# Convolution layer's input projection as seven half-size products in twelve of sixteen blocks

## The chip, the cores and the metric

The kernel runs on one core of one Trainium2 chip. The metric is the device time of one execution in microseconds (us). TensorE (PE in the profile) multiplies, VectorE (DVE), ScalarE (ACT) and GpSimd (POOL) work element by element, and SyncE (SP) issues the transfers from HBM.

## The reference, cut to what matters

A model with d = 1024, an inner width of 2048 and 512 tokens runs through four mixers (pool, convolution, latent attention, pool) and then two attention and feed-forward layers. All is float32. The changed part is the input projection of the convolution mixer:

```python
def conv_mixer(xn, w_in, conv_w, w_out):
    b, c, h, z = jnp.split(xn @ w_in, 4, axis=-1)
    y = b * causal_depthwise_conv(c * h, conv_w)
    return (y * jax.nn.silu(z)) @ w_out
```

`xn` is the normed input (512 x 1024), `w_in` is 1024 x 8192, and b, c, h, z are 512 x 2048 each.

## The kernel before, in words

Activations are held feature-major: a tile is 128 features (partitions) by 512 tokens. A matrix product keeps float32 accuracy with three matmuls: each operand is split into a rounded high part (type fp32r) and a remainder, and `mm3` issues high x high, high x low and low x high into one PSUM bank.

The work is cut into **units**. A unit is one weight tile of 128 x 1024 float32 (512 KB): eight k-blocks of 128 x 128, for 128 output features. In the convolution layer, block i (of 16) makes 128 features of each of c, h, b and z with four units, `("cc", i)`, `("ch", i)`, `("cb", i)`, `("cz", i)`; each is eight k-steps of three matmuls 512 columns wide. Eight units of `out_proj("co", 0)` follow block 7, and eight of `out_proj("co", 1)` follow block 15.

Each engine runs its own program in a fixed order, and counting semaphores join them (`at(...)` names the result that is awaited, `mark(...)` the one that is announced). Four programs carry a unit's weights, each by a function `weights(n)` that makes every unit up to n in order:

- SP loads unit n into one of four `raw` tiles; it waits until the remainder of the unit that held the tile is made (`wlo`). SP's queue is in order.
- ACT copies `raw` to the high part `WH[n % 3]` (line 1133); it waits for the transfer and until PE has finished unit n - 3 (`wfree`), because there are three weight buffers.
- DVE subtracts, raw - WH, into `WL[n % 3]` (line 1837).
- PE waits for that before the unit's first matmul.

`taking(key)` calls `weights(unit[key] + 2)`: while PE works on unit n, ACT and DVE make unit n + 2. So the high part of unit n + 2 can begin when PE begins unit n, and whatever stands ahead of the call in the program of ACT or DVE comes first.

The element work of a convolution block: DVE makes CD = c x r^2 (r is the norm's factor per token), then `("ch", i)` = h x CD; ACT scales it by the third tap into CV; DVE adds the two shifted taps (`cv0`); POOL multiplies CV by r (`cv`, line 2759); DVE multiplies b in (`cb`), makes z x r (`czr`); ACT applies Silu; POOL multiplies the two (`czy`, line 2764); ACT and DVE split the result into `YH` and `YL` for the output projection. In block 1 to 3 DVE also makes the rotary angles (`positions`, `angle`), and ACT their sines in block 5.

A layer that comes later, the second feed-forward product (`quarter`), already uses seven products in place of eight, with `PRODUCTS`, `CHAIN_OF` and `ROWS_T`.

Of the kernel before, what the change touches and what calls it, by code (L numbers as in the profile page):

```python
# [9 lines left out]
F32R = mybir.dt.float32r  # L10
I32 = mybir.dt.int32
ALU = mybir.AluOpType
# [3 lines left out]
S = 512  # L16
# [55 lines left out]

FF_ORDER = (0, 4, 1, 5, 2, 6, 3, 7)
# [12 lines left out]
SEMS = ("xin0", "xin1", "xin2", "xin3", "xin4", "xin5", "xin6", "xin7", "consts", "vec", "raw0", "raw1", "raw2", "raw3", "pos", "lam", "cos", "sin", "fn", "out",  # L86
# [48 lines left out]
def unit_table(D):  # L135

    units, index, lows = [], {}, False

    def add(key, src, ncol, dup=False):
        index[key] = len(units)  # L140
        units.append([src, ncol, dup])
# [22 lines left out]
    for i2 in range(8):  # L164
        for i in (2 * i2, 2 * i2 + 1):
            for off, nm in ((16, "cc"), (32, "ch"), (0, "cb"), (48, "cz")):
                add((nm, i), D["conv_in"][0, off + i], 1024)
        if i2 % 4 == 3:
            out_units("co", D["conv_out"], i2 // 4)
# [53 lines left out]
    loaded = [n for n, u in enumerate(units) if not isinstance(u[0], tuple)]  # L223
    slots = {n: (i % NRAW, loaded[i - NRAW] if i >= NRAW else None) for i, n in enumerate(loaded)}
    return units, index, slots
# [75 lines left out]
def program(nc, D, out):  # L301
    ctx = ExitStack()
    with ctx:
        def sb(name, cols, dt=F32, parts=128):
            return ctx.enter_context(nc.sbuf_tensor(name, [parts, cols], dt))
# [24 lines left out]
        raw = [sb(f"raw{i}", WN) for i in range(NRAW)]  # L330
# [18 lines left out]
        units, unit, slots = unit_table(D)  # L349
# [63 lines left out]
        def weight_source(n):  # L413
            src, ncol = units[n][0:2]
            if isinstance(src, tuple):
# [15 lines left out]
        def pe_program(handle, c):  # L431
# [44 lines left out]
            def xgemm(st, *key, first=False, norm=None):  # L476
                gemm8(key, XH, XL, (lambda k: ("xl", st, k)) if first else None, norm)
# [100 lines left out]

            def conv_layer():
                for i2 in range(8):  # L580
                    for i in (2 * i2, 2 * i2 + 1):
                        xgemm(1, "cc", i, first=i == 0)
# [530 lines left out]
        def act_program(handle, c):  # L1113
# [127 lines left out]
            def conv_layer(done):  # L1241
                for i2 in range(8):
                    for i in (2 * i2, 2 * i2 + 1):
                        taking("cc", i)
                        if i == 0:
                            root(1, 1024)
                        taking("ch", i)
                        act.wait_ge(*at("ch", i))
                        if i > 1:
                            act.wait_ge(*at("cb", i - 2))  # L1250
                        act.do.activation(CV[i % 2], temp("ch", i), ACT.Copy, scale=vcol("conv_w2", i)).then_inc(
                            *mark("act", ("cv2", i)))
                        taking("cb", i)
                        taking("cz", i)
                        t = temp("cz", i)
                        act.wait_ge(*at("czr", i))
                        act.do.activation(t, t, ACT.Silu).then_inc(*mark("act", ("czs", i)))
                        y_high("co", i // 8, i % 8, t, ("czy", i))
                        if i == 5:
                            sines()  # L1260
                    if i2 % 4 == 3:
                        out_proj("co", i2 // 4, done if i2 == 7 else None)

# [548 lines left out]
        def dve_program(handle, c):  # L1812
# [64 lines left out]
            def out_proj(name, rb, st=None, first=0):  # L1877
                for m in range(first, 8):
                    taking(name, rb, m)
                    add_out(m, (name, rb, m), ("x", name, rb, m) if st is None else ("x", st, m))  # L1880
                    if st is not None and st != "mid" and st < 8:
# [76 lines left out]
            def conv_layer():  # L1958
                for i2 in range(8):
                    for i in (2 * i2, 2 * i2 + 1):  # L1960
                        taking("cc", i)
                        if i == 0:
                            recip_root(1, R[:, :])
                            dve.wait_ge(*mine())
                            dve.do.tensor_tensor(CR2, R[:, :], R[:, :], ALU.mult).then_inc(*mark("dve", ("r2",)))
                        dve.wait_ge(*at("mm", "cc", i))
# [9 lines left out]
                        a = CV[i % 2]  # L1976
                        dve.wait_ge(*at("cv2", i))
                        dve.do.scalar_tensor_tensor(a, shifted(("ch", i), 1), vcol("conv_w1", i), a, ALU.mult,
                                                    ALU.add).then_inc(*mark("dve"))
                        dve.wait_ge(*mine())  # L1980
                        dve.do.scalar_tensor_tensor(a, shifted(("ch", i), 2), vcol("conv_w0", i), a, ALU.mult,
                                                    ALU.add).then_inc(*mark("dve", ("cv0", i), ("tfree", "ch", i)))
                        taking("cb", i)
                        dve.wait_ge(*at("mm", "cb", i))
                        dve.wait_ge(*at("cv", i))
                        if i > 1:
# [6 lines left out]
                        low(YL[i % 8][:, :], t, YH[i % 8][:, :], ("yh", "co", i // 8, i % 8),  # L1993
                            ("yl", "co", i // 8, i % 8), ("tfree", "cz", i))
                        if i == 1:
                            positions()
                        if i == 2:
                            angle("sin", SIN[:, :], 0.0, 0.0)
                        if i == 3:
                            angle("cos", COS[:, :], 0.25, math.pi / 2)  # L2000
                    if i2 % 4 == 3:
                        out_proj("co", i2 // 4, 2 if i2 == 7 else None)
# [677 lines left out]
        def pool_program(handle, c):  # L2680
# [72 lines left out]
            def conv_layer():  # L2753
                for i2 in range(8):
                    for i in (2 * i2, 2 * i2 + 1):
                        taking("ch", i)
                        pool.wait_ge(*at("cv0", i))
                        pool.wait_ge(*at("rstd", 1))
                        pool.do.tensor_tensor(CV[i % 2], CV[i % 2], R[:, :], ALU.mult).then_inc(*mark("pool", ("cv", i)))
                        taking("cz", i)  # L2760
                        t = temp("cz", i)
                        pool.wait_ge(*at("czs", i))
                        pool.wait_ge(*at("cb", i))
                        pool.do.tensor_tensor(t, t, CB[i % 2], ALU.mult).then_inc(*mark("pool", ("czy", i)))
                        if i == 6:
                            pool.wait_ge(*at("sin"))
                            pool.do.tensor_scalar(SIN[:, :], SIN[:, :], const[:, C_SGN:C_SGN + 1], None,
                                                  ALU.mult).then_inc(*mark("pool", ("sinr",)))
                    if i2 % 4 == 3:
                        out_proj("co", i2 // 4, 2 if i2 == 7 else None)  # L2770
# [149 lines left out]
        def sp_program(handle, c):  # L2920
# [4 lines left out]
            def weights(n):  # L2925
                while made[0] <= min(n, len(units) - 1):
                    k = made[0]
                    made[0] += 1
                    src, ncol, _, _ = units[k]
                    if isinstance(src, tuple):  # L2930
                        continue
                    slot, before = slots[k]
                    if before is not None:
                        sp.wait_ge(*at("wlo", before))
                    sp.do.dma_start(raw[slot][:, 0:ncol], src).then_inc(*mark(f"raw{slot}", ("raw", k), by=16))
# [208 lines left out]
```

## Time and profile before

| | before |
|---|---|
| median of three runs | 2676.91 us (2676.52 to 2676.93) |
| profiled execution, its own time | 2678.12 us |
| span of its profile | 2676.3 us |
| mean granted TensorE clock | 0.998 |
| convolution layer's projection, one block | 21.76 us, 16 blocks |

The span goes from the first to the last instruction. Busy times of matmuls overlap, since matmuls are pipelined: the record of a 512-column matmul is 0.39 us long, but the next one starts 0.23 us after it. So the distance from start to start is what a matmul costs.

### The profile page before, as it was taken

The numbers are of one execution on the slowest core, as the hardware profiler recorded it, in microseconds if no ns is written. First come the engines' busy times: TensorE is split into PE (matmuls) and PEld (weight loads), VectorE is DVE, ScalarE is ACT, GpSimd is POOL, SyncE is SP. The second block draws the span as 40 slices with busy tenths as digits, with TensorE's granted clock in tenths as the row PEclk, the third lists the DMA queues.
The fourth block names the chain that finished last, engine by engine and source line by source line (L and its number), as shares of the span: only waits on it lengthen the run. The fifth ranks groups of instructions, "written<-read, shape, count | busy, mean of one in ns | idle before, by whom it ended". The sixth has DMA issues, their size and how long they took to land.

```text
span 2676.3 us, 32512 instructions
## 1 busy us (share of the span) xinstructions
PE 2652.0 (99%) x12772; PEld 2222.6 (83%) x12772; DVE 1703.9 (64%) x2604; ACT 1272.0 (48%) x2002; POOL 651.6 (24%) x688
## 2 busy tenths in 40 slices
PE   8999999999999999999999999999999999999998
PEld 7888888888888888888888888788888888788887
DVE  7656554344466646666574768776677468776677
ACT  4323332222346636533235677654445677654445
POOL 1000111011126626500003744420000554420000
PEclk9999999999999999999999999999999999999999
DMA  4222222222221222222222221354551221255540
GB/s 161 98 99 98 90 103 102 95 95 95 96 68 63 68 88 66 79 87 105 95 100 97 79 72 40 105 141 148 173 158 42 80 64 48 97 152 153 173 142 32
DMA packets 76841, 263.98 MB, mean 99 GB/s; under 512 B 8976, under 2 KB 11536, under 8 KB 76688
## 3 DMA queue, kind: packets, MB, share of 16 engines
q1 hardware_dynamic: 71568, 245.12, 26.7%
q0 software_dynamic: 5120, 16.78, 3.7%
q8 instruction: 101, 1.65, 0.2%
q14 instruction: 52, 0.43, 0.0%
HBM read 259.77 MB, written 2.10 MB: 98 GB/s over the span
## 4 chain that ended last, share of the span: by engine, by line
PE 91%; DVE 4%; ACT 2%; POOL 2%; issue 0%; DMA 0%; SPq 0%; ACTq 0%; DVEq 0%
PE ps L454 27%; PE ps L455 26%; PE ps L456 26%; PE ps L460 2%; PE ps L459 2%; PE ps L461 2%; POOL wl L2707 2%; PE ps L595 1%; PE ps L857 1%; PE ps L856 1%; DVE wl L1837 1%; ACT wh L1133 0%; DVE xl L1849 0%; PE ps L528 0%; ACT xh L1144 0%
## 5 line engine op out<-in xcount | busy, mean ns | idle before, releaser
L454 PE MATMUL ps<-xh,wh 128*128 128x512 f32 x1920 | 752.2, 392 | 0.1
L455 PE MATMUL ps<-xl,wh 128*128 128x512 f32 x1920 | 748.1, 390 | 0.0
L456 PE MATMUL ps<-xh,wl 128*128 128x512 f32 x1920 | 748.0, 390 | 0.0
L1133 ACT ACTIVATE wh<-raw 128x1024 fp32r<-128x1024 f32 (+3 forms) x389 | 397.6, 1023 | 474.4 <-PE ps L456 434.9
L454 PEld LDWEIGHTS ps<-xh,wh 128*128 128x128 f32 x1920 | 361.0, 188 | 77.0 <-issue 1.2
L456 PEld LDWEIGHTS ps<-xh,wl 128*128 128x128 f32 x1920 | 360.9, 188 | 75.3
L455 PEld LDWEIGHTS ps<-xl,wh 128*128 128x128 f32 x1920 | 361.0, 188 | 74.7 <-issue 1.0
L1837 DVE TENSOR_TENSOR wl<-raw,wh 128x1024 fp32r<-128x1024 f32 (+1 forms) x275 | 339.6, 1235 | 119.9 <-ACT wh L1133 119.9
L2707 POOL TENSOR_TENSOR wl<-raw,wh 128x256 fp32r<-128x256 f32 x408 | 315.3, 806 | 405.5 <-ACT wh L1133 405.5
L454 PE MATMUL ps<-yh,wh 128*128 128x512 f32 x640 | 251.1, 392 | 1.5 <-POOL wl L2707 1.5
L456 PE MATMUL ps<-yh,wl 128*128 128x512 f32 x640 | 249.2, 389 | 0.0
L455 PE MATMUL ps<-yl,wh 128*128 128x512 f32 x640 | 249.1, 389 | 0.0
L2716 POOL TENSOR_TENSOR acc<-acc,t 128x512 f32<-128x512 f32 x52 | 72.9, 1403 | 679.7 <-ACT t L1154 677.4
L1133 ACT ACTIVATE wh<-a 128x1024 fp32r<-128x1024 f32 x96 | 101.9, 1062 | 126.8 <-PE ps L456 64.4
L1845 DVE TENSOR_TENSOR yl<-t,yh 128x512 fp32r<-128x512 f32 (+1 forms) x148 | 101.5, 687 | 78.2 <-ACT yh L1142 78.2
L454 PEld LDWEIGHTS ps<-yh,wh 128*128 128x128 f32 x640 | 120.2, 188 | 28.6 <-POOL wl L2707 3.2
L456 PEld LDWEIGHTS ps<-yh,wl 128*128 128x128 f32 x640 | 120.1, 188 | 25.2
L1142 ACT ACTIVATE yh<-t 128x512 fp32r<-128x512 f32 (+1 forms) x148 | 86.4, 585 | 114.3 <-DVE t L1949 56.3
L455 PEld LDWEIGHTS ps<-yl,wh 128*128 128x128 f32 x640 | 120.2, 188 | 23.9
L1874 DVE TENSOR_TENSOR x<-ps,x 128x512 f32<-128x512 f32 x96 | 65.6, 688 | 116.9 <-PE ps L456 116.9
L1837 DVE TENSOR_TENSOR wl<-a,wh 128x1024 fp32r<-128x1024 f32 x96 | 117.3, 1221 | 32.1 <-ACT wh L1133 32.1
L2827 POOL DMA_DIRECT2D wsum<-in_ff2t x32 | 27.2, 976 | 328.7 <-DMA wsum<-in_ff2t 322.8
(307 smaller groups left out, 4755.3 us busy)
## 6 DMA issues: line engine op xcount, KB each, us to landing
raw<-in_pool_in SPq DMA_DIRECT2D x64, 512.0 KB, 3.2
raw<-in_conv_in SPq DMA_DIRECT2D x64, 512.0 KB, 3.2
raw<-in_ff SPq DMA_DIRECT2D x64, 512.0 KB, 6.2
a<-in_ff2t SPq DMA_DIRECT2D x64, 512.0 KB, 6.9
raw<-in_pool_out SPq DMA_DIRECT2D x32, 512.0 KB, 3.2
raw<-in_qk SPq DMA_DIRECT2D x32, 512.0 KB, 3.5
raw<-in_pool_grp SPq DMA_DIRECT2D x16, 512.0 KB, 3.2
raw<-in_conv_out SPq DMA_DIRECT2D x16, 512.0 KB, 3.2
```

Of the source, the lines that this page charges most:

```text
L454: pe.do.matmul(o, lh, rh_, start=start, stop=False)
L455: pe.do.matmul(o, lh, rl_, start=False, stop=False)
L456: return pe.do.matmul(o, ll, rh_, start=False, stop=stop)
L459: pe.do.matmul(o, lh, rh_, start=False, stop=False, skip_group_check=True)
L460: pe.do.matmul(o, lh, rl_, start=False, stop=False, skip_group_check=True)
L1133: act.do.activation(h[:, 0:ncol], r[:, 0:ncol], ACT.Copy).then_inc(*mark("whi", ("whi", k)))
L1142: act.do.activation(dst, src, ACT.Copy).then_inc(*mark("act", done))
L1837: dve.do.tensor_tensor(lo[:, 0:ncol], r[:, 0:ncol], f(h[:, 0:ncol]), ALU.subtract).then_inc(*mark("wlo", ("wlo", k)))
L1845: dve.do.tensor_tensor(dst, src, f(h), ALU.subtract).then_inc(*mark("dve", *done))
L1874: dve.do.tensor_tensor(x[m][:, :], ps(*key)[:, :], x[m][:, :], ALU.add).then_inc(*mark("dve", ("psfree",) + key, *done))
L2707: p = pool.do.tensor_tensor(lo[:, cc], r[:, cc], f(h[:, cc]), ALU.subtract)
L2716: pool.do.tensor_tensor(ACC[:, :], ACC[:, :], temp("sq", use, k), ALU.add).then_inc(*mark("pool", ("acc", use, k), ("tfree", "sq", use, k)))
```

## The change

In the blocks of `CONV_BLOCKS` (2 to 6, 8 to 14) the four units become two **pairs**, (c, h) and (b, z). A pair is a product with a 2 x 2 block structure: the weights are four pieces of 512 rows x 128 features, the activations four pieces of 512 features x 256 tokens. Seven products of half size replace eight. They use sums of weight pieces and sums of activation pieces:

- The activation sums are the same for all blocks. They are made once, in blocks 0 and 1, in four steps k: ACT scales two x tiles into `COS` and `SIN` (`x_scaled`), POOL makes four sums of 256 columns and a negation (`t_sums`), ACT and DVE split the 1024 columns (`t_high`, `t_low`) into `TC[k]`.
- The weight sums are made by POOL for each block and pair: four additions 512 columns wide (`w_sums`), one block ahead, into `SW[p]`.
- A pair's products come in four weight units: (Q1, Q2) from a raw tile, (Q6, W5) and (Q7, Q3) from the two halves of `SW[p]`, and Q4 from half a raw tile. Each product is four k-steps of three matmuls of 256 columns. The units of the two pairs alternate: eight weight units a block, called s0 to s7 below.
- Products accumulate in chains in PSUM (Q1, Q6, Q7, Q4 in one bank; W5, Q3 beside Q2 in another). Between them ACT copies out partial sums (`ca1`, `ca2`, `cc1`) and DVE adds (`third_sum`, `upper`), which gives c, h, b and z scaled (`lower`).
- Per block SP still loads four tiles of 512 KB. Two more raw tiles, `RX`, serve from block 3 to block 15.
- The tap, Silu and y work of such a block moves into the next block's steps. `positions` and `angle` move into `out_proj("co", 0)`, and the sines behind it.

```diff
+CONV_BLOCKS = (2, 3, 4, 5, 6, 8, 9, 10, 11, 12, 13, 14)
+CONV_PAIRS = ((16, 32), (0, 48))
+CONV_PARTS = (("Q1", "Q2"), ("Q6", "W5"), ("Q7", "Q3"), ("Q4",))
```

ACT's program for a block of seven products, and for blocks 0, 1, 7 and 15:

```diff
+            def seven(i):
+                late = i - 1 in CONV_BLOCKS
+                for s in range(8):
+                    if s == 1:
+                        first_sum(i, 0)
+                    if s == 2:
+                        first_sum(i, 1)
+                    if s in (3, 4):
+                        second_sums(i, s - 3)
+                    if late and s == 0:
+                        tap(i - 1)
+                    if late and s == 1:
+                        gate(i - 1)
+                    weights(unit["cp", i, s % 2, s // 2] + LOOK)
+                    if late and s == 4:
+                        y_out(i - 1)
...
+            def eight(i):
+                late = i - 1 in CONV_BLOCKS
+                taking("cc", i)
+                if i == 0:
+                    root(1, 1024)
+                if late:
+                    tap(i - 1)
+                    gate(i - 1)
+                if i == 1:
+                    t_high(1)
+                    x_scaled(2)
+                taking("ch", i)
+                if late:
+                    y_out(i - 1)
+                tap(i)
+                if i == 1:
+                    t_high(2)
+                    x_scaled(3)
+                taking("cb", i)
+                if i == 0:
+                    x_scaled(0)
+                taking("cz", i)
+                if i == 0:
+                    t_high(0)
+                    x_scaled(1)
+                if i == 1:
+                    t_high(3)
+                gate(i)
+                y_out(i)
```

DVE's program for a block of seven products:

```diff
+                def seven(i):
+                    late = i - 1 in CONV_BLOCKS
+                    for s in range(8):
+                        if late and s == 0:
+                            lower(i - 1, 1, 1)
+                            lower(i - 1, 1, 0)
+                        if late and s == 1:
+                            taps(i - 1)
+                        if late and s == 2:
+                            gated(i - 1)
+                        if s == 5:
+                            third_sum(i, 0)
+                            upper(i, 0)
+                            both_scaled(i)
+                        if s == 6:
+                            third_sum(i, 1)
+                            lower(i, 0, 1)
+                        if s == 7:
+                            lower(i, 0, 0)
+                            upper(i, 1)
+                        weights(unit["cp", i, s % 2, s // 2] + LOOK)
+                        if late and s == 4:
+                            y_out(i - 1)
```

POOL's weight sums, and its order:

```diff
+                def w_sums(i, p):
+                    s2, s1, s3, s4 = [SW[p][:, 512 * n:512 * n + 512] for n in range(4)]
...
+                    pool.do.tensor_tensor(s1, b[:, 0:512], b[:, 512:1024], ALU.add).then_inc(
+                        *mark("pool", ("ws1", i, p)))
...
+                    pool.do.tensor_tensor(s3, a[:, 0:512], b[:, 0:512], ALU.add)
+                    pool.wait_ge(*at("ws1", i, p))
+                    pool.do.tensor_tensor(s2, s1, a[:, 0:512], ALU.add).then_inc(*mark("pool", ("ws", i, p, 0)))
+                    pool.wait_ge(*at("ws", i, p, 0))
+                    pool.do.tensor_tensor(s4, s2, a[:, 512:1024], ALU.add).then_inc(*mark("pool", ("ws", i, p, 1)))
+
+                for i in range(16):
+                    if i - 1 in CONV_BLOCKS:
+                        taps(i - 1)
+                        gated(i - 1)
+                    if i not in CONV_BLOCKS:
+                        taps(i)
+                    if i < 2:
+                        t_sums(2 * i)
+                    if i == 1:
+                        t_sums(3)
+                    if i not in CONV_BLOCKS:
+                        gated(i)
+                    if i == 0:
+                        t_sums(1)
+                    if i + 1 in CONV_BLOCKS:
+                        for p in range(2):
+                            w_sums(i + 1, p)
```

## Rows read from the trace of the kernel before

**Rows 1.** The page, busy time of each engine over the span.
```profile
PE 2652.0 (99%) x12772; PEld 2222.6 (83%) x12772; DVE 1703.9 (64%) x2604; ACT 1272.0 (48%) x2002; POOL 651.6 (24%) x688
```

**Rows 2.** Windows: one convolution block; columns PE, PEld, DVE, ACT, POOL busy, clock, DMA.
```profile
599.36:621.12 21.76, 21.76 (x98) 18.02 (x97) 9.69 (x11) 6.01 (x7) 3.50 (x2) 1.00 0.28 97
```

**Rows 3.** Timeline, PE, matmuls of 512 columns: start, length, engine, line.
```profile
359.96 0.39 PE L454 MATMUL ps<-xh,wh 128*128 128x512 f32 x1
...
360.64 0.39 PE L454 MATMUL ps<-xh,wh 128*128 128x512 f32 x1
```

**Rows 4.** Timeline, PE, first and last of 36 matmuls of 256 columns.
```profile
1461.73 0.28 PE L454 MATMUL ps<-wh,xh 128*128 128x256 f32 x1
...
1465.93 0.28 PE L456 MATMUL ps<-wh,xl 128*128 128x256 f32 x1
```

**Rows 5.** Timeline at the start of a unit: PE's first matmul, then ACT, DVE.
```profile
207.13 0.39 PE L454 MATMUL ps<-g,wh 128*128 128x512 f32 x1
...
207.39 1.06 ACT L1133 ACTIVATE wh<-raw 128x1024 fp32r<-128x1024 f32 x1 [3.86 <-PE ps L456]
...
208.48 1.23 DVE L1837 TENSOR_TENSOR wl<-raw,wh 128x1024 fp32r<-128x1024 f32 x1 [0.46 <-ACT wh L1133]
```

**Rows 6.** Timeline, convolution block 1, from the end of ("ch", 1).
```profile
349.28 0.69 DVE L1974 TENSOR_TENSOR t<-ps,s 128x512 f32<-128x512 f32 x1 [2.71 <-PE ps L456]
350.00 0.72 ACT L1251 ACTIVATE s<-t,vec 128x512 f32<-128x512 f32 x1 [5.04 <-DVE t L1974]
...
351.55 0.75 DVE L1981 SCALAR_TENSOR_TENSOR s<-t,vec,s 128x512 f32<-128x512 f32 x1
352.21 1.22 DVE L1837 TENSOR_TENSOR wl<-raw,wh 128x1024 fp32r<-128x1024 f32 x1
352.38 2.21 POOL L2759 TENSOR_TENSOR s<-s,r 128x512 f32<-128x512 f32 x1 [10.43 <-DVE s L1981]
...
361.59 1.29 POOL L2764 TENSOR_TENSOR t<-t,s 128x512 f32<-128x512 f32 x1 [7.00 <-ACT t L1257]
```

**Rows 7.** Timeline, end of the first pool layer: GpSimd and VectorE together.
```profile
301.25 1.30 POOL L2716 TENSOR_TENSOR acc<-acc,t 128x512 f32<-128x512 f32 x1 [4.15 <-ACT t L1154]
...
301.82 1.28 DVE L1849 SCALAR_TENSOR_TENSOR xl<-x,vec,xh 128x512 fp32r<-128x512 f32 x1 [1.31 <-ACT xh L1144]
```

**Rows 8.** Timeline, first attention layer: GpSimd without a gap, VectorE behind it.
```profile
1501.64 2.83 POOL L2707 TENSOR_TENSOR wl<-raw,wh 128x256 fp32r<-128x256 f32 x4
...
1502.79 8.47 DVE L1845 TENSOR_TENSOR ptl<-s,pth 128x384 fp32r<-128x384 f32 x3
```

**Rows 9.** One line's instructions: count, shortest/median/longest ns, first and last start.
```profile
L1849 DVE SCALAR_TENSOR_TENSOR xl<-x,vec,xh x56: 744/1269/1866, 7.6 to 2341.5; 128x512 fp32r<-128x512 f32 x56
```

**Rows 10.** Groups by line and shape: count, busy us, mean ns.
```profile
L1845 DVE TENSOR_TENSOR ptl<-s,pth 128x384 fp32r<-128x384 f32 x64 | 46.3, 757 | 5.3 <-ACT pth L1142 5.3
...
L2543 DVE TENSOR_TENSOR tsum<-t 128x256 f32<-128x256 f32 x32 | 13.3, 417 | 0.0
...
L1282 ACT ACTIVATE s<-ps,small 128x256 f32<-128x256 f32 x32 | 15.2, 486 | 0.0
...
L2778 POOL TENSOR_SCALAR s<-s,small 128x256 f32<-128x256 f32 x16 | 15.0, 938 | 0.0
```

**Rows 11.** Timeline, convolution block 0, first half of its element work.
```profile
333.43 1.99 ACT L1133 ACTIVATE wh<-raw 128x1024 fp32r<-128x1024 f32 x2
...
335.18 2.21 POOL L2759 TENSOR_TENSOR s<-s,r 128x512 f32<-128x512 f32 x1 [16.32 <-DVE s L1981]
335.44 1.28 ACT L1257 ACT_TABLE_LOAD   x1
```

**Rows 12.** Windows with a low granted clock (the column after POOL).
```profile
1627.00:1630.00 3.00, 3.00 (x18) 2.47 (x18) 2.97 (x9) 2.97 (x7) 0.00 (x0) 0.50 0.00 0
...
2668.00:2676.00 8.00, 0.39 (x2) 0.00 (x0) 2.95 (x6) 3.47 (x8) 0.00 (x0) 0.70 0.56 211
```

**Rows 13.** The page, transfers by kind: count, KB each, us to landing.
```profile
raw<-in_conv_in SPq DMA_DIRECT2D x64, 512.0 KB, 3.2
```

More of the change, by code:

```diff
@@ L135, in unit_table, with add @@
 def unit_table(D):
-    units, index, lows = [], {}, False
-    def add(key, src, ncol, dup=False):
+    units, index, loads, wide, narrow = [], {}, [], [], []
+    def add(key, src, ncol, dup=False, load=True):
         index[key] = len(units)
+        if load and not isinstance(src, tuple):
+            loads.append(len(units))
         units.append([src, ncol, dup])
@@ L165, in unit_table @@
         for i in (2 * i2, 2 * i2 + 1):
+            if i in CONV_BLOCKS:
+                for j in range(4):
+                    for p, (first, second) in enumerate(CONV_PAIRS):
+                        part = (D["conv_in"][0, first + i], ("S", i, p, 0), ("S", i, p, 1),
+                                D["conv_in"][0, second + i])[j]
+                        add(("cp", i, p, j), part, 512 if j == 3 else 1024, load=j == 0)
+                if i == CONV_BLOCKS[1]:
+                    wide.append(len(loads))
+                loads.extend(index["cp", i, p, j] for p, j in ((0, 0), (1, 0), (0, 3), (1, 3)) if j == 3)
+                continue
             for off, nm in ((16, "cc"), (32, "ch"), (0, "cb"), (48, "cz")):
@@ L222, in unit_table @@
         u.append(on)
-    loaded = [n for n, u in enumerate(units) if not isinstance(u[0], tuple)]
-    slots = {n: (i % NRAW, loaded[i - NRAW] if i >= NRAW else None) for i, n in enumerate(loaded)}
-    return units, index, slots
+    queue, holder, slots = list(range(NRAW)), {}, {}
+    for i, n in enumerate(loads):
+        if i in wide:
+            queue = [NRAW, NRAW + 1] + queue
+        if i in narrow:
+            queue = [q for q in queue if q < NRAW]
+        q = queue.pop(0)
+        queue.append(q)
+        slots[n] = q, holder.get(q)
+        holder[q] = n
+    return units, index, slots, loads
 def temp_table():
@@ new lines, in y_out, with x_scaled @@
+                def y_out(i):
+                    y_high("co", i // 8, i % 8, temp("cz", i), ("czy", i))
+                def x_scaled(k):
+                    if k:
+                        act.wait_ge(*at("tcs", k - 1))
+                    for dst, m in ((COS, k), (SIN, k + 4)):
+                        act.wait_ge(*at("x", 1, m))
+                        a = act.do.activation(dst[:, :], x[m][:, :], ACT.Copy, scale=vcol("conv_norm", m))
+                    a.then_inc(*mark("act", ("xg", k)))
@@ new lines, in t_high, with first_sum @@
+                def t_high(k):
+                    if k == 0:
+                        act.wait_ge(*at("mm", "grp", 0, 3, 3))
+                    high(TC[k][:, 0:1024], RX[k % 2][:, :], ("tcs", k), ("tch", k))
+                def first_sum(i, p):
+                    o = CB[i % 2] if p else CD
+                    if p and i > 1:
+                        act.wait_ge(*at("czy", i - 2))
+                    if not p:
+                        act.wait_ge(*at("ch", i - 1))
+                    act.wait_ge(*at("mm", "c", i, p, "Q1"))
+                    act.do.activation(o[:, 0:256], ps("cA", i, p)[:, 0:256], ACT.Copy).then_inc(
+                        *mark("act", ("ca1", i, p)))
@@ L1253, in conv_layer @@
[L1253 to L1260, printed above, removed]
+                        if i in CONV_BLOCKS:
+                            seven(i)
+                        else:
+                            eight(i)
@@ L1875, in add_out, with out_proj @@
                     *mark("dve", ("psfree",) + key, *done))
-            def out_proj(name, rb, st=None, first=0):
+            def out_proj(name, rb, st=None, first=0, between={}):
                 for m in range(first, 8):
```

247 lines of the change are left out of this document (197 added, 50 removed).

## The prediction, made before the changed kernel was run

> **What bounds the kernel now.** I read the page's busy times first: PE is busy over 99% of the span, GpSimd 24% [rows 1]. Then a window of one convolution block: PE is busy for all of its 21.76 us, VectorE for 9.69, ScalarE for 6.01, GpSimd for 3.50, at full clock [rows 2]. So this layer is bound by PE's stream of matmuls, and a saving counts only while the helpers keep up. Then the timeline for what a matmul costs from start to start: 512 columns take (360.64 - 359.96) / 3 = 0.2267 us [rows 3], and 256 columns (1465.93 - 1461.73) / 35 = 0.120 us [rows 4]. Half the columns cost 53%, not 50%.
>
> **The gain on PE.** A block had 4 x 24 = 96 matmuls of 512 columns, 96 x 0.2267 = 21.76 us, as the window has it [rows 2, 3]. It gets 2 pairs x 7 products x 12 = 168 of 256 columns, 168 x 0.120 = 20.16 us [rows 4]. That is 1.60 us a block and **-19.2 us** for twelve. Twelve and a half per cent of the columns go, but only 7% of the time.
>
> **What the helpers get to do.** From start to start a 1024-wide `wl` costs DVE about 1.14 us and a 512-wide operation 0.6 (their records overlap a little), a 256-wide one 0.42 [rows 6, 10]. Per new block DVE has six `wl` of 1024 and two of 512, two taps, `cd`, the gating, `y_out`, and eight short operations on PSUM or `lower`: some 14 us. ScalarE has six copies at 1.06, two half ones, six PSUM copies at under 0.49 [rows 5, 10], and three others: under 13 us. Neither fills 20.16. GpSimd goes from two operations to ten: eight weight sums at 1.29 [rows 6] are 10.3 us, 12.9 with the old two. It has room too, if taken alone.
>
> **They can't be taken alone.** In block 1 the POOL product L2759 lasts 2.21 us, and L2764, of the same shape, 1.29. The first began 0.17 us after a DVE `wl` of 1.22 [rows 6]: it waited for that one's end, 1.05 us, and then ran 1.16. The other way round: a DVE `xl` that needs 0.744 at its fastest takes 1.28 when it meets a POOL addition that began 0.57 before [rows 7, 9]: 0.73 of waiting until 302.55, then 0.55. And in the attention layer three DVE subtractions, of a kind whose mean is 0.76, take 8.47 us together while POOL runs without a gap [rows 8, 10]. So here a DVE operation with two SBUF inputs and a POOL operation run one after the other, never at once.
> The Trainium skill ("SBUF — State Buffer", section "Who interferes with whom") says the same: a VectorE instruction with two SBUF inputs contends with a GpSimd instruction that reads SBUF, and the later one blocks fully; one with a PSUM input doesn't. The traces agree, with the 2.21 against 1.29 us above. By that rule no overlap may be counted; without it the sum would be the first rival's.
>
> Count what excludes itself per block. DVE: six `wl` at 1.1, two at 0.57, two taps at 0.65, `cd`, gating and `y_out` at 0.57, two `lower` halves at 0.33: about 11.4 us. POOL: ten at 1.16 to 1.25: about 12. Together 23.4 us, against 20.16 of PE and 21.76 before. That alone makes a fully loaded block slower than before.
>
> I laid one such block out, PE's s0 at 0, with steady lateness. DVE: `lower` of the pair before and `wl` of s2 until 3.95, taps until 5.35, `wl` s3 6.4; POOL's tap product until 7.55, gating 8.25, `wl` s4 9.3; POOL's gating 10.45, `wl` s5 11.55; two weight sums until 13.95 (the second was ready when DVE's next high part came), `wl` s6 14.5, a sum 15.65, `y_out` 16.2, PSUM sums 17.2 under the fourth weight sum, `cd` 17.9, a sum 19.05, `wl` s7 19.6, `third_sum` of the second pair 19.95. PE wanted that last one for Q4 at 18.72 and waits 1.3 us. Then a sum 20.75, `lower` 21.1, a sum 22.25 and `wl` of the next s0 23.35: PE wanted it at 21.5, and waits 1.9. So a loaded block takes 23.35 to 23.5 us, **3.3 over its 20.16**. The cause of the tight place: Q4's two units are 1.44 us each, so the weights for s0 must be made in 2.88 us, and undisturbed they take 208.48 + 1.23 - 207.13 = 2.58 [rows 5]. One POOL sum ahead of them breaks that.
> Loaded are blocks 3, 4, 5 and 9 to 13: 8 x 3.3 = **+26.4 us**. Blocks 6 and 14 have no weight sums beside them, and block 8's DVE has no work of a block before: +0.2 each, +0.6. Bounds per loaded block: from the exclusive sum without any idle time with the shortest holds (22.5, +2.3) to a POOL that wins several times running, as in rows 8 (26.5, +6.3).
>
> **The way in.** The activation sums and the first weight sums stand in ScalarE's and GpSimd's queues ahead of work that PE waits for. By times of the old trace:
> (1) POOL's tap product ends at 337.4 [rows 11]. `t_sums(0)` is four 256-wide operations at 2.83 / 4 = 0.71 [rows 8] and a negation at 0.94 [rows 10], with two own waits some 4.0 us, plus one `wl` met (1.1): 342.5. `t_high(0)` 1.06 and `x_scaled(1)` 2 x 0.7: 344.9. The Silu table load of 1.28 [rows 11] and Silu: 346.8. POOL's gating and `y_out(0)`: 348.8. Only now ScalarE makes the high part of `("cb", 1)`; its remainder, past a POOL operation, is there at 351.5. PE wants it at 349.1: **2.4**.
> (2) `t_sums(1)` stands behind the gating: 354.1; `t_high(1)`, `x_scaled(2)`, then the weights of `("cz", 1)`: 358.7, wanted at 356.9: **1.8**.
> (3) DVE's h product comes behind that, the taps end at 361.6 (0.72 and twice 0.75 after it [rows 6]), POOL's product, behind `t_low(1)`, at 363.9, `t_sums(2)` 368.0, `t_high(2)` and `x_scaled(3)` 370.4, weights of block 2's s0 with one POOL wait 373.0; wanted at 364.2: **8.8**. s1: **0.7**.
> (4) `t_sums(3)` 377.6, `t_high(3)`, Silu 379.3, POOL's gating behind `t_low(3)` 381.0, three weight sums past one `y_out` 385.4, copy and remainder 387.9; wanted at 379.6: **8.3**. The second pair's sums, four further with a `wl` between: 394.0, wanted at 390.8: **3.2**.
> Sum **+25.2 us**. With nothing met on the shared port and each chain only by its dependencies I get 1.0 + 1.4 + 5 + 2.2 = 9.6; with a second port wait of 1.1 us in each of the six steps some 32. I take the laid-out value, since every wait in it has its opponent.
>
> **Clock.** PE stood nearly idle at the end (0.39 of 8 us busy) and the granted clock of that stretch was 0.70; in another, after small matmuls, it was 0.50, which is 1.2 of 2.4 GHz [rows 12]. Two standstills of over 8 us may do this. Most of the slow time would lie ahead of a further wait; I take **+2**, bounds 0 and 7.
>
> **What costs nothing.** The angles move to out_proj units, where DVE has 1.9 us of work in 5.44 (unit = 24 x 0.2267) and is two units ahead; without that cover they cost under 5 us each. The sines follow them, ahead of s2's weights only. SP issues as many loads as before; a first tile is held until POOL's fourth sum, and the two further raw tiles cover this from block 3 on. In block 2 it delays block 3's last loads to 392.9 (the end of the last weight sum for block 2) and the 3.2 us of a load [rows 13], about 396; the sums that want them belong to block 3. PSUM: four banks of eight a block.
>
> **Sum.** -19.2 + 26.4 + 0.6 + 25.2 + 2 = +35.0. The profiled execution took 2678.1 around a span of 2676.3, 1.2 above the median of 2676.9; a difference is not touched by that. 2676.9 + 35.0 = **2712 us**.
>
> **Rivals.**
> (a) *The saving counts, the additions hide*: POOL's weight sums fall into DVE's waits on PE, and only the dependencies of the way in cost. 2676.9 - 19.2 + 9.6 = 2667. For it: DVE is idle for over 5 us of a block. Against: 23.4 us of exclusive work in 20.16. It decides the sign if the port costs under (19.2 - 9.6) / 8 = 1.2 us a loaded block. 0.10.
> (b) *The two cancel*: port at its lower bound and way in near its own, within 5.4 us of before. 0.05.
> (c) *Slower, about as laid out*, 2683 to 2735: 0.68.
> (d) *Runaway*: POOL wins repeatedly, or the waits of 3 us a block bring the clock down in every block (3 us more in each of 8 to 11): 2735 to 2765. 0.17. For it: rows 8. Against: DVE mostly gets its turn at the next boundary.
>
> Faster by over 0.2% 0.10, within 0.2% (about what a measurement of this kernel can tell from no change) 0.05, slower 0.85. Range 2680 to 2750, which leaves out (a), part of (b) and the top of (d); the likeliest case's own is 2690 to 2730.
>
> **What would show it.** PE's 256-column matmuls 0.120 apart; POOL's weight sums with spans over 1.29 and DVE's `wl` over 1.23 in loaded blocks; PE idle before s0 and s7 of blocks 3 to 5 and 9 to 13, released by DVE; gaps of over 5 us before block 2's s0 and s2, released by ScalarE's or DVE's weights behind POOL. I am wrong if the loaded blocks take under 21.8 us, or if block 2 starts on time.

## The result and the profile after

The changed kernel takes 2709.22 us (median of four, 2708.47 to 2711.82) against 2676.92 (2676.52 to 2677.28) of the kernel before: a ratio of 1.0122, 95% interval 1.0105 to 1.014. The forecast was 2712, in a range of 2680 to 2750, and slower at 0.85.

The page of the changed kernel answers to [rows 1]. PE has slack that it did not have, and GpSimd went from 24% to 31%. Of the 40 slices below (67.7 us each) the sixth to the eleventh are the convolution layer: GpSimd's digits there are 6, 8, 3, 5, 8, 4, and TensorE's clock has its only digit below 9 in the sixth.

```profile
PE 2640.8 (98%) x13636; PEld 2251.4 (83%) x13636; DVE 1849.6 (68%) x2728; ACT 1341.7 (50%) x2134; POOL 845.3 (31%) x804
...
PE   8999978998999999999999999999999999999998
...
POOL 1000168358426644610001754230000544330000
PEclk9999989999999999999999999999999999999999
```

The windows of one loaded block (block 5) and one light block (6) stand against [rows 2]; the columns are as there, with the number of instructions in brackets.

```profile
453.10:476.50 23.40, 20.63 (x168) 20.26 (x168) 22.14 (x22) 11.12 (x17) 19.09 (x11) 1.00 0.27 91
476.50:496.70 20.20, 20.15 (x168) 20.15 (x169) 17.35 (x22) 11.13 (x17) 7.65 (x4) 1.00 0.33 105
```

The light block shows what the change was to give: 168 matmuls in 20.2 us, where 21.76 were needed. In the loaded one the same 168 take 23.40, VectorE has a record open for 22.14 of them, and GpSimd for 19.09. Blocks 4, 5 and 10 to 13 are alike, at 23.4 to 23.5; block 3 took 24.2 and block 9 22.3.

What PE waited for over the whole run (total in us, times, longest in us), the first three rows; none of them has a counterpart before:

```profile
PE ps L489 <- DVE wl L1997: 25.3, 13, 8.2
PE ps L494 <- DVE t L2141: 9.2, 7, 1.7
PE ps L494 <- DVE wl L1997: 7.2, 2, 6.7
```

Line 1997 makes the weights' remainder, 2141 is `third_sum`; 489 opens a product on `xh` (s0, s1, and the units of blocks of eight), 494 one on the activation sums.

The timeline of the loaded block on VectorE and then on GpSimd (start, length):

```profile
462.58 3.46 DVE L1997 TENSOR_TENSOR wl<-sw,wh 128x1024 fp32r<-128x1024 f32 x2
465.95 1.78 DVE L1997 TENSOR_TENSOR wl<-raw,wh 128x512 fp32r<-128x512 f32 x1
467.66 1.78 DVE L2005 TENSOR_TENSOR yl<-t,yh 128x512 fp32r<-128x512 f32 x1
469.36 0.41 DVE L2141 TENSOR_TENSOR t<-ps,t 128x256 f32<-128x256 f32 x1
...
471.06 1.78 DVE L1997 TENSOR_TENSOR wl<-raw,wh 128x512 fp32r<-128x512 f32 x1
472.77 0.41 DVE L2141 TENSOR_TENSOR t<-ps,t 128x256 f32<-128x256 f32 x1
...
474.20 2.30 DVE L1997 TENSOR_TENSOR wl<-raw,wh 128x1024 fp32r<-128x1024 f32 x1
```

```profile
464.91 2.27 POOL L3040 TENSOR_TENSOR sw<-rx 128x512 f32<-128x512 f32 x1
467.15 1.74 POOL L3045 TENSOR_TENSOR sw<-raw,rx 128x512 f32<-128x512 f32 x1
468.85 1.74 POOL L3047 TENSOR_TENSOR sw<-sw,raw 128x512 f32<-128x512 f32 x1
470.67 1.63 POOL L3049 TENSOR_TENSOR sw<-sw,raw 128x512 f32<-128x512 f32 x1
472.26 1.72 POOL L3040 TENSOR_TENSOR sw<-rx 128x512 f32<-128x512 f32 x1
473.96 1.45 POOL L3045 TENSOR_TENSOR sw<-raw,rx 128x512 f32<-128x512 f32 x1
475.37 2.27 POOL L3047 TENSOR_TENSOR sw<-sw,raw 128x512 f32<-128x512 f32 x1
```

GpSimd has seven operations without a gap. VectorE's 512-wide `wl` and `yl` have records of 1.78 us each, one behind the other at distances of 1.71 us. In the first version below, in which GpSimd reads nothing, the same two start 0.61 apart (435.46 and 436.07). So each stands some 1.1 us, about the length of one GpSimd sum. `third_sum`, with an input in PSUM, keeps its 0.41. The last `wl` here is the one of the next s0: it starts at 474.20 and lasts 2.30, and PE, which wanted it 1.7 us sooner, begins at 476.55.

### The profile page after: what moved, and what is told of

Same layout as the page of the kernel before. It is cut to its first block, busy times and chain, and to the rows that moved or that the text cites. A ratio compares the mean times of both kernels' runs of the same rounds, so it can differ in the third digit from the quotient of the medians.

```text
span 2707.2 us, 34682 instructions
## 1 busy us (share of the span) xinstructions
PE 2640.8 (98%) x13636; PEld 2251.4 (83%) x13636; DVE 1849.6 (68%) x2728; ACT 1341.7 (50%) x2134; POOL 845.3 (31%) x804
## 3 DMA queue, kind: packets, MB, share of 16 engines
q1 hardware_dynamic: 71568, 245.12, 27.2%
## 4 chain that ended last, share of the span: by engine, by line
PE 81%; DVE 11%; POOL 4%; ACT 3%; issue 1%; DMA 0%; SPq 0%; ACTq 0%; DVEq 0%; POOLq 0%
PE ps L489 23%; PE ps L491 23%; PE ps L490 23%; DVE wl L1997 4%; PE ps L494 2%; PE ps L496 2%; PE ps L495 2%; POOL wl L2958 2%; PE ps L671 1%; DVE t L2162 1%; POOL s L3008 1%; DVE yl L2005 1%; ACT wh L1209 1%; PE ps L933 1%; PE ps L932 1%
## 5 line engine op out<-in xcount | busy, mean ns | idle before, releaser
L489 PE MATMUL ps<-xh,wh 128*128 128x512 f32 (+1 forms) x1728 | 658.3, 381 | 25.4 <-DVE wl L1997 25.3
L490 PE MATMUL ps<-xl,wh 128*128 128x512 f32 (+1 forms) x1728 | 652.9, 378 | 0.0
L491 PE MATMUL ps<-xh,wl 128*128 128x512 f32 (+1 forms) x1728 | 652.8, 378 | 0.0
L1209 ACT ACTIVATE wh<-raw 128x1024 fp32r<-128x1024 f32 (+3 forms) x369 | 369.8, 1003 | 437.1 <-PE ps L491 364.6
L1997 DVE TENSOR_TENSOR wl<-raw,wh 128x1024 fp32r<-128x1024 f32 (+1 forms) x255 | 329.6, 1293 | 121.9 <-ACT wh L1209 121.9
L489 PEld LDWEIGHTS ps<-xh,wh 128*128 128x128 f32 x1728 | 325.9, 189 | 89.9 <-DVE wl L1997 28.5
L491 PEld LDWEIGHTS ps<-xh,wl 128*128 128x128 f32 x1728 | 325.8, 189 | 60.4
L490 PEld LDWEIGHTS ps<-xl,wh 128*128 128x128 f32 x1728 | 326.0, 189 | 59.5 <-issue 1.0
L2005 DVE TENSOR_TENSOR yl<-t,yh 128x512 fp32r<-128x512 f32 (+1 forms) x148 | 111.0, 751 | 45.8 <-ACT yh L1218 45.8
```

The source lines that it names most:

```text
L489: pe.do.matmul(o, lh, rh_, start=start, stop=False)
L490: pe.do.matmul(o, lh, rl_, start=False, stop=False)
L491: return pe.do.matmul(o, ll, rh_, start=False, stop=stop)
L1209: act.do.activation(h[:, 0:ncol], r[:, 0:ncol], ACT.Copy).then_inc(*mark("whi", ("whi", k)))
L1997: dve.do.tensor_tensor(lo[:, 0:ncol], r[:, 0:ncol], f(h[:, 0:ncol]), ALU.subtract).then_inc(*mark("wlo", ("wlo", k)))
L2005: dve.do.tensor_tensor(dst, src, f(h), ALU.subtract).then_inc(*mark("dve", *done))
```

## Experiments

All times are medians; the kernel before ran beside each at 2676.6 to 2677.7.

**Without the weight sums.** The sums for all blocks but 2 and 8 are left out; in place of each stand two fills of its destination, so that these products are formed with constants.

```diff
-                    pool.do.tensor_tensor(s1, b[:, 0:512], b[:, 512:1024], ALU.add).then_inc(
-                        *mark("pool", ("ws1", i, p)))
+                    fill(s1, ("ws1", i, p))      # two memsets; so for s3, s2, s4
```

> GpSimd's weight sums for blocks 3 to 6 and 9 to 14 are left out: two fills of the same tile with a constant stand for each addition, so their semaphores, the order of the queue and the writes stay, and only the reads of SBUF go (the weights of Q6, W5, Q7 and Q3 are then wrong in these blocks). If VectorE and GpSimd exclude each other because both read SBUF: the loaded blocks fall from 23.4 us to 20.2 to 20.5, and the time by about 25 us to 2684 (2681 to 2688). If the waits before s0 and s7 come from VectorE's own load or from the short Q4 units alone: the blocks stay at 23.4 and the time within 3 us of 2709.

2682.06 us, ratio 1.0018 (1.0008 to 1.0027). A loaded block (window of block 4) is at PE's own time:

```profile
432.00:452.16 20.16, 20.16 (x170) 20.16 (x170) 14.98 (x21) 11.37 (x19) 12.33 (x19) 1.00 0.33 106
```

All waits from block 3 on are gone, and those of the way in are as they were. So 27 us, the difference of the two medians, is what the 80 additions cost against two fills each, though GpSimd is no busier than 31% of the run. The groups by form from block 3 to block 14, of the changed kernel and then of this one (count, busy, mean ns):

```profile
L1997 DVE TENSOR_TENSOR wl<-sw,wh 128x1024 fp32r<-128x1024 f32 x44 | 64.2, 1477 | 6.5 <-ACT wh L1209 6.5
L1997 DVE TENSOR_TENSOR wl<-raw,wh 128x512 fp32r<-128x512 f32 x14 | 21.0, 1498 | 1.7 <-ACT wh L1209 1.7
L2141 DVE TENSOR_TENSOR t<-ps,t 128x256 f32<-128x256 f32 x22 | 9.1, 412 | 0.0
```

```profile
L1997 DVE TENSOR_TENSOR wl<-sw,wh 128x1024 fp32r<-128x1024 f32 x44 | 53.7, 1220 | 15.9 <-ACT wh L1209 15.9
L1997 DVE TENSOR_TENSOR wl<-raw,wh 128x512 fp32r<-128x512 f32 x14 | 9.6, 689 | 8.6 <-ACT wh L1209 8.6
L2141 DVE TENSOR_TENSOR t<-ps,t 128x256 f32<-128x256 f32 x22 | 9.2, 419 | 0.0
L3035 POOL MEMSET sw<- 128x512 f32 x72 | 37.9, 526 | 4.1
```

The operation with a PSUM input is the same in both. The 512-wide one goes from 1498 to 689 ns. The fills, with no input, did not hold VectorE up: its 1024-wide `wl` took 1220 ns beside them, and 1477 beside the sums.

**The last sums held back.** GpSimd's three last sums of a block wait until the remainder of the next s0 is made.

```diff
                     pool.wait_ge(*at("raw", first))
+                    if p and before is not None:
+                        pool.wait_ge(*at("wlo", unit["cp", i, 0, 0]))
```

> Nothing left out. The last three weight sums of a block wait until the remainder for the next block's s0 is made, so none of them can stand ahead of it. If the exclusive work as a total bounds a loaded block (23.4 us of it by the layout, 22.5 at the least), the waits only move: 22.5 to 23.4 us a block, 2702 to 2709. If the loss is one badly placed sum ahead of the weights of s0: that wait of 1.7 us goes in every loaded block, 21.7 us a block, 2694 to 2697.

2711.2 us, ratio 1.0126 (1.011 to 1.0141): no change. The block is still 23.4 long. The waits moved: 1.88 before s7, 0.63 before s0, 0.37 before s2, where there were 1.4 before s7 and 1.7 before s0. So it is not the one sum ahead of s0's weights that sets the block. The result is what a bound by the total of exclusive work asks for; that this total is 23.4 us is the forecast's estimate.

**The sums on VectorE.** The same four additions a pair in VectorE's program, behind the weights calls of s2, s3, s4 and s5, one block ahead.

```diff
                         weights(unit["cp", i, s % 2, s // 2] + LOOK)
+                        if s == 2 and i + 1 in CONV_BLOCKS:
+                            w_sums(i + 1, 0, 0)      # dve.do.tensor_tensor: s1, s3
```

> Nothing left out. VectorE makes the weight sums of blocks 3 to 6 and 9 to 14, GpSimd only those of blocks 2 and 8. If exclusion is the cause: exclusive work is then about 16.0 us of VectorE and 2.4 of GpSimd, 18.4 in all, and VectorE's whole work 14 + 8 x 0.6 = 18.9; a block takes 20.3 to 21.5 us, the time falls by 15 to 25 us, to 2684 to 2694. If VectorE's own load is the cause, five more us of it make the loaded blocks longer than 23.4, and the time rises to 2715 or more.

2700.95 us, ratio 1.0089 (1.0074 to 1.0104). A loaded block takes 22.0, not the 20.3 to 21.5 expected, and its only wait is 1.8 before s7, on `third_sum`. Another place was tried, the last two sums behind the weights call of s7:

> Nothing left out. As the run in which VectorE makes the weight sums, with the last two of a block behind the remainder for s1 instead of ahead of the third sum of the second pair. In that run the only wait left in a loaded block was 1.8 us before the second pair's Q4 (22.0 us a block). If it comes from that order: 20.2 to 20.6 us a block, the time falls by 11 to 14 us from 2701, to 2687 to 2690. If VectorE is full with 19 us of work (or GpSimd's two products still collide): the wait moves elsewhere, 21.5 us a block or more, 2696 or more.

2698.61 us, ratio 1.008 (1.0063 to 1.0097): missed as well, and again exactly 22.0 a block, now with 1.0 before s6 and 0.76 before s7. The window of a loaded block, and two rows of VectorE's timeline in it:

```profile
448.10:470.10 22.00, 20.61 (x168) 20.27 (x168) 20.67 (x31) 11.08 (x18) 4.37 (x2) 1.00 0.30 96
```

```profile
458.55 0.69 DVE L2174 TENSOR_TENSOR s<-s 128x512 f32<-128x512 f32 x1 [1.19 <-POOL s L3034]
...
460.29 1.79 DVE L2183 TENSOR_TENSOR sw<-rx 128x512 f32<-128x512 f32 x1
```

VectorE has 31 operations in the window. Its only idle time is the 1.19 ahead of the gating, which waits for GpSimd's tap product, and the sum at 460.29 stands 1.1 behind GpSimd's gating product. 22.0 - 1.2 - 1.1 = 19.7 is its own work. By this reading VectorE itself is the bound once the sums are moved: 19.7 fits into PE's 20.16 only if it stands for GpSimd no longer than 0.5 us a block. No run took work away from VectorE alone to show it.

**Half and half.** Pair one's sums on VectorE, pair two's on GpSimd.

> Nothing left out. VectorE makes the weight sums of the first pair, GpSimd those of the second (blocks 3 to 6 and 9 to 14). Exclusive work is then 11.4 + 2.3 of VectorE and six operations of GpSimd, 7.2: 20.9 us, between 23.4 and 18.4. If the loss grows with the exclusive total: 21.0 to 22.0 us a loaded block, 2690 to 2698. If every second operation of GpSimd would already do the harm, by its place: 23 us or more, 2706 to 2710.

2716.94 us, ratio 1.0147 (1.0132 to 1.0162): worse than either, against an expected gain. The eight loaded blocks took 22.8 to 24.9 us (the longest with some of the slow clock in them), though the exclusive work was put at 20.9. Waits of 1.7 to 2.7 stand before s6 and 0.75 before s7, and the clock fell five times in the loaded blocks. VectorE's timeline shows why:

```profile
440.29 1.22 DVE L1997 TENSOR_TENSOR wl<-sw,wh 128x1024 fp32r<-128x1024 f32 x1
441.43 1.79 DVE L2183 TENSOR_TENSOR sw<-raw 128x512 f32<-128x512 f32 x1
443.14 1.78 DVE L2187 TENSOR_TENSOR sw<-rx,raw 128x512 f32<-128x512 f32 x1
...
446.69 1.68 DVE L2192 TENSOR_TENSOR sw<-sw,rx 128x512 f32<-128x512 f32 x1
```

Three of its four sums here wait for a GpSimd operation, and now they stand in VectorE's own queue ahead of the weights and of `third_sum`. A VectorE sum that costs 0.6 us alone takes 1.7 with the wait. So the total of exclusive work is the least that a block can take and not its length: where the operations stand counts too.

**The way in, reordered.** The activation sums spread over blocks 0 and 1 so that each stands behind the weights that PE wants next, and block 2's first weight sums ahead of GpSimd's gating product. Of GpSimd's program (the moves of the other `t_sums` and those on ScalarE and VectorE are left out here):

```diff
+                    if i == 1:
+                        t_sums(3)
+                        w_sums(2, 0)
                     if i not in CONV_BLOCKS:
                         taps(i)
+                    if i == 1:
+                        w_sums(2, 1)
                     if i not in CONV_BLOCKS:
                         gated(i)
```

> Nothing left out. The way in alone: the activation sums start at the head of block 0, in ScalarE's and GpSimd's idle time, ahead of the taps, and the first weight sums stand ahead of the gating of block 1; blocks 3 and later are as in the changed kernel. If the standstills before s0 and s2 of block 2 come from this order, nearly all of the 24 us by which block 3 begins later than before goes, with both drops of TensorE's clock: 2684 to 2690. If they come from the amount of work or from a transfer, less than half of it goes: over 2697.

2692.27 us, ratio 1.0058 (1.0041 to 1.0074): 17 us faster than the changed kernel, just short of the range expected. 1.50 before cz0, 0.35, 1.72 before s0 and 4.24 before s2 are left of the way in, and the clock falls once. The loaded blocks from 5 on take what they took, 23.4 us and block 9 22.3; blocks 3 and 4 take 23.3 and 22.4, about a microsecond less each.

**Both, and the first block of seven one later.** Sums on VectorE as in the late version, `CONV_BLOCKS` from 3, activation sums over blocks 0 to 2.

> Nothing left out. Three changes together: the weight sums on VectorE as in the run beside it, the first of the blocks of seven products is block 3 and not 2, and the activation sums are spread over blocks 0 to 2, one GpSimd series at a time. If the way in and the shared port are all that the change lost: block 3 begins within 3 us of its time before, eleven blocks gain 1.6 each minus 0.2, so 2676.9 - 15.4 + 3 = 2664 (2659 to 2669), faster than before. If something else costs, such as the rate of instructions or the moved angles: over 2672.

2677.9 us, ratio 1.0002 (0.9992 to 1.0011): no difference from before, where 2664 was expected. The clock never falls in the layer. The expectation took 20.2 us a block, and it is 22.0: 11 x 1.6 saved, less 8 x 1.8 and the 2.5 that stand before block 3's s2 and s3, leaves 0.7 us of saving, and the times show none.

**PE alone.** Eleven blocks, the spread way in, fills in place of the sums of all blocks but 3 and 8.

> Left out: the weight sums of all blocks but 3 and 8, with two fills in the place of each addition (so the weights of four of the seven products are wrong there). Eleven blocks of seven products from block 3 on, the way in spread. This measures the gain of PE alone: 11 x 1.6 = 17.6 less about 2.5 us of waits at the entry of block 3, 2662 (2659 to 2664). If blocks of 256-column matmuls cost more than 20.16 us in a row, over 2666.

2661.39 us, ratio 0.9942 (0.9928 to 0.9955): 15.5 less than before. With the 2.2 us of waits that are left in block 3 (2.5 by the matmuls' starts) that is 17.7 to 18.0, against 11 x 1.60 = 17.6. PE's term is right, and anything else that the change costs is under half a microsecond.

**Every second block.** Seven products in blocks 3, 5, 8, 10, 12 and 14, so that GpSimd's sums (its own again) fall into blocks in which VectorE has little to do.

```diff
+CONV_BLOCKS = (3, 5, 8, 10, 12, 14)
```

> Nothing left out. Blocks 3, 5, 8, 10, 12 and 14 have seven products, all others eight; GpSimd makes the weight sums, in the block of eight products ahead, where VectorE has 12 us to spare; the way in is spread as in the version that begins with block 3. If the shared port and VectorE's load are all that stood against the saving: six blocks at 20.2 to 20.4 us and no wait elsewhere, 2676.9 - 6 x 1.5 = 2668 (2666 to 2671), faster than before. If GpSimd's additions cost wherever they stand, or PE gains less than 1.6 us a block: 2673 or more.

2701.08 us, ratio 1.009 (1.0077 to 1.0104): missed by 33 us. Four blocks wait 0.80 before s0 and 4.24 before s2, block 3 waits 3.4, and the clock falls behind each. GpSimd's and ScalarE's timelines at the start of block 3:

```profile
381.00 2.26 POOL L3035 TENSOR_TENSOR sw<-raw 128x512 f32<-128x512 f32 x1
383.22 2.28 POOL L3040 TENSOR_TENSOR sw<-raw 128x512 f32<-128x512 f32 x1
385.46 1.28 POOL L3042 TENSOR_TENSOR sw<-sw,raw 128x512 f32<-128x512 f32 x1
386.83 1.30 POOL L3044 TENSOR_TENSOR sw<-sw,raw 128x512 f32<-128x512 f32 x1
388.08 1.28 POOL L3009 TENSOR_TENSOR t<-t,s 128x512 f32<-128x512 f32 x1
```

```profile
389.39 0.63 ACT L1218 ACTIVATE yh<-t 128x512 fp32r<-128x512 f32 x1 [3.78 <-POOL t L3009]
389.93 1.04 ACT L1209 ACTIVATE wh<-sw 128x1024 fp32r<-128x1024 f32 x1
```

The weights of s2 are not late by their sums. ScalarE stands for 3.78 us at `y_out` of the block before, which waits for a gating product that GpSimd has queued behind the sums, and nobody wants y before the output projection.

**That one step deferred.** `y_out` of a block of eight ahead of a block of seven moves behind the weights call of s4.

```diff
-                        if late and s == 4:
+                        if i != 8 and s == 4:
                             y_out(i - 1)
...
                     gate(i)
-                    y_out(i)
+                    if i == 7 or i + 1 not in CONV_BLOCKS:
+                        y_out(i)
```

> The every-second-block version with one thing moved: the splitting of y (its rounded high part on ScalarE, its remainder on VectorE) of an eight-product block that stands ahead of a seven-product block no longer ends that block's program, but stands behind s4's weights of the block that follows. Theory (ScalarE's in-order queue): the waits before s2 in blocks 3, 5, 10, 12 and 14 (3.2 to 4.2 us each) came from ScalarE standing at y, behind GpSimd's gating, behind the weight sums, and not from weight sums that were late. Then these waits go and the clock doesn't fall: 2676.9 - 6 x 1.6 + 4 x 0.8 that stand before s0 = 2670.5, 2667 to 2674. Rival (the sums are late themselves, since each is stretched by VectorE): the waits before s2 keep more than half of their length, 2685 to 2700.

2672.52 us (eleven runs), ratio 0.9983 (0.9974 to 0.9992): inside the range expected, 28.6 faster than the same kernel without the move, and the one complete version that is faster than before, by 4 us. What is left in the layer is 0.6 us of these waits in each of four blocks (0.8 to 0.9 by the matmuls' starts); ScalarE now passes:

```profile
PE ps L489 <- DVE wl L1997: 2.6, 4, 0.6
```

```profile
383.96 0.63 ACT L1328 ACTIVATE t<-t 128x512 f32<-128x512 f32 x1 [6.04 <-DVE t L2026]
384.50 1.05 ACT L1209 ACTIVATE wh<-sw 128x1024 fp32r<-128x1024 f32 x1
```

Six blocks save 9.6 and the four waits give back some 3.5, which leaves 6.1. In the traces the layer is 5.7 us shorter than before (386.5 from PE's first start in it to the first of its last output projection, against 392.2). The medians differ by 4.0; the 1.7 us between lie outside the layer and are not explained.

**GpSimd's tap product first.** To remove these last waits, the tap product stands ahead of all eight sums.

> As the deferred version, and GpSimd's tap product stands ahead of all eight weight sums of the block and not between the two pairs' sums. If the 0.8 us before s0 come from VectorE waiting for the tap product behind the first pair's sums, they go: 2667 (2665 to 2670). If the sums become late by it, a new wait stands before s2 or s3 of each of five blocks, 1 to 3 us each: 2672 to 2685.

2682.32 us, ratio 1.0021 (1.0012 to 1.003). The waits before s0 are gone and five others have come, before s2, 0.9 in block 3 and 2.34 in four blocks, as the rival had it: the sums are now the late ones.

```profile
PE ps L494 <- DVE wl L1997: 9.4, 5, 2.2
```

## Why the prediction was right, and where its terms were off

**PE's term** (-19.2) was right: 20.16 a block in the fills version, 20.2 in block 6 of the changed kernel, and 17.7 for eleven blocks in the version with PE alone.

**The exclusion** was right and is shown by taking the sums away and nothing else. The forecast laid a loaded block out at 23.35 to 23.5 us with 1.3 before s7 and 1.9 before the next s0; measured were 23.4, 1.4 and 1.7. With block 3 at 24.2 and block 9 at 22.3 (why these two differ was not looked into) the eight together are 187.0 - 8 x 20.16 = 25.7 over, against 26.4. The light blocks 6, 8 and 14 were 1.1 over, against 0.6; 0.9 of it is block 8. The Trainium skill ("SBUF — State Buffer", section "Who interferes with whom") has a VectorE instruction with two SBUF inputs contend with a GpSimd one that reads SBUF, so that the later one blocks fully, and spares a VectorE instruction with a PSUM input. The runs agree on both counts: 1498 against 689 ns, and 412 against 419.

**The cause given for the place** was too narrow. The forecast said that one sum ahead of s0's weights breaks a tight step. Holding those sums back moved the wait and did not shorten the block. The sum of 23.4 us of exclusive work was the better argument; the place was its symptom. That measured and summed length agree to 0.1 us is partly luck: with the sums split between the engines even the shortest loaded block was 1.9 us longer than its sum.

**The way in** was right in kind. The waits came where they were named, except that s1 had none and block 3's s0 had one that was not named. Here are ScalarE's rows in the two standstills, and the windows across them (PE's clock is the column after POOL):

```profile
366.93 1.06 ACT L1218 ACTIVATE tc<-rx 128x1024 fp32r<-128x1024 f32 x1 [7.69 <-POOL rx L3030]
...
369.12 1.99 ACT L1209 ACTIVATE wh<-raw 128x1024 fp32r<-128x1024 f32 x2
...
379.43 0.63 ACT L1218 ACTIVATE yh<-t 128x512 fp32r<-128x512 f32 x1 [1.92 <-POOL t L3014]
383.53 1.06 ACT L1209 ACTIVATE wh<-sw 128x1024 fp32r<-128x1024 f32 x1 [3.47 <-POOL sw L3047]
...
389.56 1.06 ACT L1209 ACTIVATE wh<-sw 128x1024 fp32r<-128x1024 f32 x1 [4.71 <-POOL sw L3047]
```

```profile
363.30:371.80 8.50, 0.37 (x2) 0.00 (x0) 1.61 (x2) 4.17 (x5) 5.94 (x8) 0.79 0.00 0
371.80:379.00 7.20, 7.16 (x47) 7.16 (x48) 5.21 (x5) 1.58 (x2) 5.34 (x4) 0.77 0.00 1
379.00:386.00 7.00, 0.31 (x4) 0.11 (x2) 2.38 (x2) 1.96 (x3) 6.92 (x6) 0.71 0.01 3
386.00:391.10 5.10, 5.10 (x24) 5.10 (x24) 0.45 (x1) 1.54 (x3) 4.81 (x4) 0.50 0.28 99
```

| PE waits before | forecast | measured |
|---|---|---|
| cb1 | 2.4 | 2.45 |
| cz1 | 1.8 | 0.48 |
| s0 | 8.8 | 8.33 |
| s1 | 0.7 | 0 |
| s2 | 8.3 | 6.85 |
| s3 | 3.2 | 0.85 |
| block 3's s0 | 0 | 1.73 |
| sum | 25.2 | 20.7 |
| clock and rest | 2 | 4.3 |
| together | 27.2 | 25.0 |

Block 3's s0 came at 405.5, 23.8 later than before. PE was already 0.35 late when the layer began (316.28 against 315.93), so the layer itself made it 23.4 late; with block 2's 1.6 of saving that is the 25.0. The row for the clock is what the waits leave of it.

The rows for s2, s3 and the clock belong together. PE worked at the lower granted clock from 371.8 to 375.1 and from 386.0 to 391.1: s0 and s1 took 1.5 us longer by it, and s2 2.3. But the weights of s2 and s3 were held by GpSimd's sums, as the rows above show, and these did not wait for PE. Without the slow clock PE would have stood before s2 for 6.85 + 1.5 = 8.4 us and before s3 for 0.85 + 2.3 = 3.2 (an estimate from these starts), and the forecast had 8.3 and 3.2. So these two terms were right, and so was the sentence that most of the slow time lies ahead of a further wait. With the two waits written so, all waits are 24.6 and the clock and the rest 0.4. The mis-sized terms are cz1 (1.3 too large), s1 (0.7, which did not come), the clock (+2, nearly all of it hidden) and block 3's s0 (1.73, put at nothing); they cancel in part, and that is luck.

**The sum**: -19.2 + 25.7 + 1.1 + 20.7 + 4.3 = 32.6. The layer is 32.9 longer in the trace, and the medians differ by 32.3. The spans differ by only 30.9. Where the layer ends the changed kernel is 33.3 behind, and it makes 2.8 us of that good at one place (PE's starts are 33.2 later near 1620 us of the kernel before and 30.4 later at 1645): the profile of before has a stretch of the lower clock near 1627 us [rows 12], and that of after has none in the same attention work.

**The rivals.** (a), that the saving counts and the additions hide, fell: that would be 2667, and the version with most of the way in mended still takes 2692. (b), that the two cancel, fell with it, since neither loss was near its lower bound. (c) came true. (d)'s own clause, the clock falling in every block, did not happen at waits of 1.4 and 1.7 us; in the half-and-half version it fell five times, behind waits of 2.5 and 2.7.

## What to carry to other kernels

Before work is given to GpSimd, add up per stage its operations on SBUF and VectorE's with two SBUF inputs as if they were one engine; if the sum is over the stage's length, the stage takes at least that sum, however idle both look on the page. Another order of the same work did not get under it here, and a bad one took longer. Moving the work to the other engine helps only if that one has room for it and for the operations that it still meets. Then look in each in-order queue for a step that nobody needs yet, standing ahead of the bound engine's next input: here moving `y_out` ahead of five blocks was worth 28.6 us, more than the whole change could have given.

## What the runs showed of the hardware

- When both engines had work, they took turns here: VectorE's 512-wide operations came every 1.71 us between GpSimd's, against 0.61 with none of GpSimd's reads beside them. The repeated wins of GpSimd seen in [rows 8] did not come back in the loaded blocks.
- GpSimd's memset, 526 ns for 128 x 512, left VectorE's 1024-wide `wl` at 1220 ns: no exclusion was seen without an input.
- A 256-column matmul started 0.120 us after the one before it at the higher granted clock, a 512-column one 0.227, so seven half-size products save 7.4% and not 12.5% of a block. At the lower clock 256 columns took 0.21 to 0.22 (s2 of block 2).
- The granted clock fell to the lower of its two levels, 1.2 of 2.4 GHz, 5.0 us after PE stopped at 363.3 and 3.0 us after it stopped at 379.0, for 6.8 and 10.2 us. The waits of 1.4 and 1.7 us in the loaded blocks, and the 2.45 at 349.2, left it at the higher one; in the version with the tap product first, one of four waits of 2.34 us was followed by 3.4 us at the lower one.
